# A two-block transformer kernel on one core: the second block's convolved keys and compressed branch moved between its token projections, and the last norm's transposes taken from unscaled rows

## The reference, cut to what matters

```
h  = rmsnorm(x, norm_mix)
(dn_qkv, dn_z, dn_b, dn_a, ns_q, ns_kc, ns_vc, ns_ks, ns_vs, ns_kw, ns_vw, ns_gate, ...) = split(h @ w_in)
qkv  = silu(causal_depthwise_conv(dn_qkv, conv_w))         # four taps; keys are one third of it
kc   = rmsnorm(gelu(blocks(ns_kc) @ w1) @ w2, kn_cmp)      # 15 compressed keys, values alike
q    = rmsnorm(ns_q, q_norm) / 8 ;  ks, kw normed alike
o_ns = gated sum of attention over compressed, selected and windowed keys
x = x + mix @ w_out
h2 = rmsnorm(x, norm_mlp)                                  # x * s * g, s one number a token
x = x + square(relu(h2 @ w_up)) @ w_down
```

## Time and profile before

| | |
|---|---|
| time, median of 3 runs | 999.0 us (997.72 to 999.48) |
| the profiled execution's own time | 1003.03 us |
| its span, first to last instruction | 1001.2 us |
| mean granted TensorE clock | 0.979 |
| PE, PEld busy | 931.7 us (93%), 826.8 us (83%) |
| DVE, ACT, POOL busy | 610.0, 465.6, 153.6 us |
| DMA | 139.60 MB, 139 GB/s on average |

### The profile page before, as it was taken

One profiled execution on the slowest core, in us unless ns is written; L12 is line 12 of the kernel. 1 busy time (PEld: TensorE's weight loads), 2 busy tenths in 40 slices (PEclk: granted clock), 3 DMA queues, 4 the chain that ended last, 5 costly groups with the idle time before them and its releaser, 6 DMA issues. The chain is left out here.

```text
span 1001.2 us, 17392 instructions
## 1 busy us (share of the span) xinstructions
PE 931.7 (93%) x6836; PEld 826.8 (83%) x6836; DVE 610.0 (61%) x1288; ACT 465.6 (47%) x906; POOL 153.6 (15%) x111
## 2 busy tenths in 40 slices
PE   4999897999999969989699999898999979999998
PEld 2997686999999959879688888897888779999996
DVE  4557656556445577459877977626756656544553
ACT  5454545535444455363334674353453445444441
POOL 2000000000000014001775314000000004222321
PEclk9999998999999989999799999999999989999999
DMA  8540332564566434363432201202546436555451
GB/s 307 166 138 1 114 118 85 169 209 164 175 193 209 156 105 139 135 252 113 162 127 86 64 13 43 86 3 85 176 160 193 146 124 207 193 190 168 169 189 42
DMA packets 38677, 139.60 MB, mean 139 GB/s; under 512 B 4330, under 2 KB 4586, under 8 KB 38596
## 3 DMA queue, kind: packets, MB, share of 16 engines
q1 hardware_dynamic: 37184, 134.17, 39.8%
q10 hardware_dynamic: 884, 2.49, 0.7%
q0 software_dynamic: 528, 1.84, 0.6%
HBM read 137.39 MB, written 1.08 MB: 138 GB/s over the span
## 5 line engine op out<-in xcount | busy, mean ns | idle before, releaser
L1642 DVE TENSOR_TENSOR parts<-raw,parts 128x1024 fp32r<-128x1024 f32 (+1 forms) x227 | 291.1, 1319 | 170.5 <-ACT parts L1166 169.2
L1166 ACT ACTIVATE parts<-raw 128x1024 fp32r<-128x1024 f32 (+1 forms) x227 | 229.8, 1048 | 114.9 <-PE psum L504 104.9
L502 PE MATMUL psum<-hT,parts 128*128 128x256 f32 (+1 forms) x928 | 265.5, 286 | 10.2 <-DVE scr L2052 9.4
L503 PE MATMUL psum<-hT,parts 128*128 128x256 f32 (+1 forms) x928 | 264.1, 285 | 0.0
L504 PE MATMUL psum<-hT,parts 128*128 128x256 f32 (+1 forms) x928 | 262.3, 283 | 0.0
L502 PEld LDWEIGHTS psum<-hT,parts 128*128 128x128 f32 x928 | 176.6, 190 | 13.3 <-DVE scr L2052 9.6
L504 PEld LDWEIGHTS psum<-hT,parts 128*128 128x128 f32 x928 | 177.6, 191 | 0.0
L503 PEld LDWEIGHTS psum<-hT,parts 128*128 128x128 f32 x928 | 176.9, 191 | 0.5
L502 PE MATMUL psum<-parts,arena_r 128*128 128x512 f32 x344 | 137.1, 399 | 3.6 <-issue 3.0
L504 PE MATMUL psum<-parts,arena_r 128*128 128x512 f32 x344 | 136.5, 397 | 0.0
L503 PE MATMUL psum<-parts,arena_r 128*128 128x512 f32 x344 | 136.4, 396 | 0.0
(11 more groups left out here) (293 smaller groups left out, 1158.4 us busy)
## 6 DMA issues: line engine op xcount, KB each, us to landing
raw<-weights SPq DMA_DIRECT2D x247, 512.0 KB, 4.2
raw<-weights SPq DMA_DIRECT2D x4, 384.0 KB, 7.9
X<-x SPq DMA_DIRECT2D x2, 512.0 KB, 6.4
out<-X SPq DMA_DIRECT2D x2, 512.0 KB, 2.6
arena<-lines POOLq DMA_DIRECT2D x1, 768.0 KB, 10.3
cbuf<-consts ACTq DMA_DIRECT2D x1, 561.0 KB, 5.3
arena<-lines POOLq DMA_DIRECT2D x1, 544.0 KB, 7.6
arena<-params ACTq DMA_DIRECT2D x1, 512.0 KB, 9.0
```

What stands on the lines that cost most here:

```text
L502: mm(ps, a, c, start=start, stop=False)
L503: mm(ps, a, d, start=False, stop=False)
L1166: signal(A(split_slot(name)[0], whole_piece, ACT.Copy), "first_parts")
L1642: signal(V_.tensor_tensor(second, whole_piece, first.bitcast(F32), ALU.subtract), "split_vector")
```

## The change

It has two parts.

**Order at the start of the second block.** The pieces, PE's jobs and the work of ACT and DVE on them stand in a new order: kvc, small, cv_k0, hid, nq0, kvc2, cv_k1, nq1, kcT, cv_k2, nk, cv_k3, nqT_0 to nqT_7, nv, nkT, cv_v0. No job is added or taken away. The pieces of each `feature_pair` get names of their own in the table, and `cmp` now stands behind `qnsa0` in it, though PE uses `cmp` ahead of `qnsa0`.

**The last norm.** `X` is transposed unscaled, four transposed tiles after the third of the four pieces of `out2_1` (`amid`) and four in the middle of the first product of up_0 (`ahead_of`). The factor s squared is applied where DVE adds the result of `w_down` to `X`. The scaled copies of the rows are gone, and the sums of squares and the root stand behind the transposed tiles.

```diff
-for _n in ["qnsa0", "qnsa1", "ksw", "cmp", "vsw", "dk0", "dk1", "dv0", "dv1", "dq0", "dq1", "z0", "z1",
+for _n in ["dk0.0", "dk0.1", "qnsa0", "cmp", "dk0.2", "dk0.3", "qnsa1", "dk1.0", "dk1.1", "ksw", "dk1.2", "dk1.3", "vsw", "dv0", "dv1", "dq0", "dq1", "z0", "z1",
...
             def feature_product(name, cols, ps, acts=hT, ahead_of={}):
                 for k in range(KD):
+                    if k in ahead_of:
+                        ahead_of[k]()
                     need(k)
...
             def token_products(unit, tiles, acts, width=512, amid=None):
+                    if j == 2 and amid:
+                        amid()
...
+            conv_half("k", 0, 0, 0)
+            compressed_hidden()
+            two_tokens("qnsa0", "nq0")
+            compressed_keys_values()
+            conv_half("k", 0, 0, 1)
+            two_tokens("qnsa1", "nq1")
+            compressed_keys_turned()
+            conv_half("k", 0, 4, 0)
             two_tokens("ksw", "nk")
+            conv_half("k", 0, 4, 1)
+            queries_turned()
             two_tokens("vsw", "nv")
+            keys_turned()
             for what in EARLY:
                 conv_half(*what)
...
+            def rows_turned(nh):
+                for t in range(TT):
+                    freed(pe, f"o2_{nh}_{t}")
+                transposes_of(X, lambda k: f"norm4_{k}", ks=range(4 * nh, 4 * nh + 4))
+
+            two_tokens("out2_0", "o2_0", mixT)
+            two_tokens("out2_1", "o2_1", mixT, lambda: rows_turned(0))
+            late_rows = {4: lambda: rows_turned(1)}
...
+                    done_with(f"up2.{2 * j}", feature_product(f"up2.{2 * j}", tok, ps[:, 0:SEQ],
+                                                              ahead_of=late_rows if j == 0 else {}))
+                    if j == 0:
+                        turn[0], turn[1] = 0, 4
...
     # ACT
+            turned_out(lambda k: f"norm4_{k}", hT, SEQ, lambda k: par("norm_mlp")[:, k:k + 1])
             half_sums("sq4", lambda t, nh: f"o2_{nh}_{t}", dn["Vb"].rearrange("p (t n) -> p t n", t=TT))
-            second_tile("4", dn["Vb"].rearrange("p (t n) -> p t n", t=TT))
-            turned_out(lambda k: f"norm4_{k}", hT, SEQ, lambda k: par("norm_mlp")[:, k:k + 1])
...
     # DVE
+            for nh in range(2):
+                residual([(t, nh, f"o2_{nh}_{t}") for t in range(TT)], nh == 0)
+                turned_rest(lambda k: f"norm4_{k}", hT, SEQ, lambda k: par("norm_mlp")[:, k:k + 1], range(4 * nh, 4 * nh + 4))
+            dve.wait_ge(sem("sq4"), 2 * TT)
...
+                    release(V_.scalar_tensor_tensor(out=xs, in0=bank_of(name), scalar=st[:, 10 + t:11 + t], in1=xs,
+                                                    op0=ALU.mult, op1=ALU.add), name)
```

More of the change, by code:

```diff
@@ L880, in z_half, with compressed_hidden @@
                 two_tokens(f"z{n}", f"z{n}")
+            blk = nsa["blk"].rearrange("p (s l n) -> p s l n", s=2, l=16)
+            Q = nsa["Q"].rearrange("p (t n) -> p t n", t=TT)
+            ksw = nsa["ksw"].rearrange("p (t n) -> p t n", t=TT)
+            def compressed_hidden():
+                u = [whole(f"cmp.{n}").rearrange("p (l n) -> p l n", n=P) for n in range(4)]
+                freed(pe, "kvc_0")
+                freed(pe, "kvc_1")
+                ps = opened("hid")
+                for s in range(2):
+                    for l in range(16):
+                        last = mm(ps[:, 64 * s:64 * s + 60], u[2 * s + l // 8][:, l % 8, :], blk[:, s, l, :], start=(l == 0), stop=(l == 15))
+                closed(last, "hid")
+                for n in range(4):
+                    piece_used[f"cmp.{n}"] = "hid"
@@ new lines, in compressed_keys_values @@
+            def compressed_keys_values():
+                freed(pe, "hid")
+                ps = opened("kvc2")
+                for s in range(2):
+                    for g in range(NSG):
+                        slot = g if s else 2 * (g % 2) + g // 2
+                        last = mm(ps[0:NC, 256 * s + 64 * slot:256 * s + 64 * slot + 64], hid[:, s, 15 * g:15 * g + 15],
+                                  par("w2k" if s == 0 else "w2v"), start=True, stop=True)
+                closed(last, "kvc2")
@@ new lines, in compressed_keys_turned, with queries_turned @@
+            def compressed_keys_turned():
+                ps = opened("kcT")
+                pe.wait_ge(sem("kc_norm"), 1)
+                for s in range(2):
+                    last = nc.tensor.transpose(ps[:, 16 * s:16 * s + NC], kcn[0:NC, P * s:P * s + P], ident[0:NC, 0:NC])
+                closed(last, "kcT")
+            def queries_turned():
+                pe.wait_ge(sem("nq_norm"), 2)
+                for k in range(KD):
+                    name = f"nqT_{k}"
+                    ps = opened(name)
+                    for t in range(TT):
+                        last = nc.tensor.transpose(ps[:, P * t:P * t + P], Q[:, t, P * k:P * k + P], ident)
+                    closed(last, name)
@@ new lines, in keys_turned @@
+            def keys_turned():
+                pe.wait_ge(sem("nk_norm"), 2)
+                for b in range(2):
+                    name = f"nkT_{b}"
+                    ps = opened(name)
+                    for s in range(2):
+                        for t in range(TT):
+                            src = ksw[:, t, 256 * b + P * s:256 * b + P * s + P]
+                            at = SEQ * s + P * t
+                            last = nc.tensor.transpose(ps[:, at:at + P], src, ident)
+                    closed(last, name)
@@ L897, in _ @@
-            closed(last, "hid")
-            for n in range(4):
-                piece_used[f"cmp.{n}"] = "hid"
-            two_tokens("vsw", "nv")
[L901 to L935, removed]
@@ L2056, in _ @@
+            inv_rms(st[:, 80:96], st[:, 64:80], ND, st[:, 128:144], st[:, 160:176])
+            for t in range(TT):
+                v = nsa["ksw"][:, 512 * t:512 * t + 512].rearrange("p (h d) -> p h d", d=ND)
+                signal(V_.tensor_tensor(v, v, bc(st[:, 80 + 8 * t:88 + 8 * t], [P, 8, ND]), ALU.mult), "nk_norm")
+            convolve("k", 0, 4, 1)
             for what in EARLY:
```

158 lines of the change are left out of this document (73 added, 85 removed).

## The result

The changed kernel takes 1012.56 us (median of 4 runs, 1010.77 to 1015.32), the kernel before 998.95 beside it (4 runs, 997.72 to 999.48): 1.0135 times as long, 95% interval 1.0114 to 1.0156. So it is slower by 13.6, where 2.4 was forecast. The profiled execution took 1011.77 with a span of 1009.9, against 1003.03 and 1001.2 before: +8.7 from trace to trace.

The account below looks back on a forecast made before the run. PE, busy 93% of the span, was taken as the bound, through its idle time and clock. Old waits -15.6, new waits +23.1 (+7.5), last norm -5.1: +2.4 on the median 999.0 gives 1001.4, range 996.5 to 1007.

Parts of the forecast that it names:

- The list of waits, old and new: Second block's start: old waits 2.66 and 9.40 go; new 5.7 before hid, 6.5 before cv_k1, 5.6 at nqT_7 come.
- waits 2 and 3: Wait 2: before cv_k1, for DVE's split of `dk0.2`, 6.5 plus 1.9 of clock; wait 3 has its own line.
- The last norm: Second part of the forecast: transposing `X` unscaled around out2_1 and up_0 saves 5.1, with up_1 waiting for the Relu.
- The sign: Whole kernel: forecast slower, by +2.4; chances slower 0.52, same 0.32, faster 0.16.
- POOL would not slow the chain's last splits: DVE's last two splits before bank 0 is released: priced 2.35, not 5.45 beside POOL, which would add 3.1.
- wait 3: At nqT_7, for bank 0 until DVE's convolution of cv_k3 ends: 5.6, and nv behind it loses 1.65.
- hid has the slow clock (1.7): Behind wait 1 of 5.7, hid was to take 7.25 + 1.7, losing only 1.7 to the low clock.
- The rival: Hid at half clock throughout: hid takes twice 7.25 and nq0 loses 1.65, 8.9 instead of 1.7, 1008.6; chance 0.12.
- the 5.30: Old wait in the last norm, behind the scaling of line 1693; 16 transposes after it take 3.65 instead of 1.97.
- Sum: Closing step: +7.5 - 5.1 = +2.4, from the profiled execution's 1003.03 to 1005.4, but put on the median 999.0: 1001.4.

Follow-up runs that it names:

- hid_wide: Changed kernel with hid's matmuls 256 columns wide in place of 60, same number of instructions, output not the reference's; 1011.17 us (one run).
- cmp_mid: Changed kernel with the `cmp` pieces loaded and split between `qnsa0.1` and `qnsa0.2`, one table line; 989.71 us, ratio 0.9884 to the kernel before.
- hid_behind_nq0: Changed kernel with nq0 made between the wait for the four `cmp` pieces and hid; 1006.33 us, ratio 1.0061 to the kernel before.
- hid_thrice: Changed kernel with hid's matmuls done three times over, same output; 1042.01 us (one run).
- before_again: The kernel before, unchanged, measured and profiled once more; 1000.47 us, ratio 1.0001, its profiled execution 999.39.

## Why the prediction was wrong

**Right.** The list of waits, old and new, their places and what ends them: 5.99, 6.43 and 5.26 against 5.7, 6.5 and 5.6, and none ahead of cv_v1. The low clock behind waits 2 and 3: cv_k1 lost 1.8 (7.56 against 5.8) and nv 1.6 (12.81 against 11.18), as taken. The second of these has luck in it: behind the same wait of 5.2 to 5.3, the same matmuls of nv took 12.74 to 14.23 in seven kernels with the new order, so that they lost between 1.6 and 3.1. The longest is that of hid_wide:

```profile
480.17:494.40 14.23, 14.23 (x51) 11.35 (x52) 4.81 (x4) 5.09 (x6) 2.40 (x2) 0.78 0.45 149
```

The last norm: -4.9 alone against -5.1, with 0.69 ahead of up_1. The sign. That POOL would not slow the chain's last splits: wait 3 came out 0.3 shorter with 2.35 a pair, not 3.1 longer.

**The step that failed** is "hid has the slow clock (1.7)": a term that was mis-sized, with the right mechanism written down as a rival. 1.7 was read from matmuls of 512 columns behind a wait and put on matmuls of 60. Measured, hid loses 13.88 - 7.25 = 6.6 and nq0 behind it another 12.96 - 11.20 = 1.8, 8.4 in all: 6.7 more than taken. The rival had it at 8.9 and was given 0.12. What spoke against it, 1021 small matmuls from 640 to 690 at 1.00, was evidence on another question: they show that narrow matmuls keep a full clock, which cmp_mid shows of hid too. The trace before had no matmuls of 60 columns behind a wait, and its nearest rows point two ways. Behind the 5.30, the 16 transposes of 128 columns ran at the half clock all the way, and the wide matmuls behind them had the full clock almost at once (0.97 from 816.08 to 822.10), so that a fixed loss fits:

```profile
812.56:816.08 3.52, 3.52 (x16) 3.25 (x17) 2.24 (x6) 2.82 (x7) 0.00 (x0) 0.50 0.00 0
```

Behind the 13.52 with which the span begins, small matmuls, most of them transposes, run until 23.0. Still the 272-column matmuls behind them (and behind 0.82 more of idle time) go at half pace to about 27.9 and double it only then. The clock column reads 1.00 there, so this is read from their lengths:

```profile
24.19 0.43 PE L503 MATMUL psum<-hT,parts 128*128 128x272 f32 x1
...
28.41 0.29 PE L502 MATMUL psum<-hT,parts 128*128 128x272 f32 x1
```

With such rows the two ends should have had nearly equal chances, and the range should have reached to the far end. hid_behind_nq0, hid_thrice and hid_wide settle it. With the 6.7 the profiled execution would have been forecast at 1005.4 + 6.7 = 1012.1; it took 1011.77.

**The second step** is the one in "Sum" that puts a difference between traces on the median of the runs. The trace before held a wait of 9.40, which two other profiles with the same order have at 6.47 and 6.29, so a change that takes it away is worth 2.9 less in a usual execution than in that one. The trace's being 4.0 above the median was the warning: where in the trace the 4.0 stood had to be asked, since part of it lay in the wait that the change takes out.

The two make 9.6 of the 11.2 by which the time was missed. Put on the forecast they give 2.4 + 6.7 + 2.9 = 12.0, and from the end of small to the end of the span the changed kernel's trace is 11.9 longer than before_again's. So these traces leave next to nothing open there. The remaining 1.6 of the medians is not assigned: the four runs of the changed kernel are spread over 4.5, and the end of small alone moves by 4.7 from trace to trace. Why DVE's pairs of splits take 10.7 beside POOL in one execution and 7.6 in another was seen, not tried; the turns above fit it.

## What to carry to other kernels

A wait on TensorE has two prices, its own length and the low clock of what follows. For waits of some 6 the second was, here, as much again as hid's narrow matmuls take at the full clock (6.6) plus what the first wide ones lose (1.6 to 3.1 of a job of 48). Put wide products behind a wait that can't be avoided. And before a small job is moved forward, look at where the splits and loads that it and its successor need stand in the other engines' queues: here an order of matmuls that costs 15.5 gains some 6 (989.71 - 1000.59 = -10.9, of which the last norm is -4.9) once `cmp` stands two pieces earlier in a table. If a profiled execution lies off the median, find in it the place of the difference before a gain is counted from that place.

## What the runs showed of the hardware

Matmuls of 60 columns, one behind another without a gap, behind a wait of 6.2, left the granted clock at 0.50 for 41.6 us (hid_thrice); the same matmuls without a wait ahead of them had 1.00 from the first to the last (7.25, cmp_mid). With 256 columns the clock was back at 1.00 within hid, so that four times the columns cost 0.25 over hid and nq0 together. That they cost so little is the clock's doing alone: at one and the same clock the wide ones take twice as long, 0.213 against 0.113 (7.25/64) from one start to the next at the full clock, and 0.44 against 0.217 (13.88/64) at the half clock. In hid's window at half clock the weight loads are busy as long as the matmuls (13.88 each). Widths between 60 and 256 were not tried.
